# Lag and length of a scan's software pipeline: halves seven steps apart, outputs in step 11 of 13

## The chip, the cores and the metric

The kernel runs on one core of a Trainium2 chip. A core has TensorE (matrix products, into PSUM), VectorE, ScalarE and GpSimd (POOL in the profile), and SyncE, which here only issues the loads of weights. Each engine works through its own program in order; semaphores order the engines against each other. The metric is the device time of one execution in microseconds, lower is better.

## The reference

One hybrid layer over 512 tokens, then two layers over 512 + 256 tokens, all in float32. The hybrid layer mixes two kinds of attention with a gated linear attention (GLA). Each of the two later layers mixes a Fourier branch, an attention of 8 heads over 2 key-value heads, and a gated recurrence that runs forward and backward:

```python
def hgrn_scan(k, v, log_f, s0, q=None):
    # S_t = diag(f_t) S_{t-1} + k_t v_t^T, o_t = S_t^T q_t, chunk by chunk
    def step(s, inp):
        kc, vc, lf = inp[0], inp[1], inp[2]
        cum = jnp.cumsum(lf, axis=2)
        last = cum[:, :, -1:, :]
        s_new = jnp.exp(last[:, :, 0, :])[..., None] * s + \
            jnp.einsum('bhsd,bhse->bhde', kc * jnp.exp(last - cum), vc)
```

The outputs of a chunk are a part within the chunk (masked scores times values) and a part from the state that comes into it (queries times state).

## The kernel before

The program is a row of stages. The large products (`gemm_*`, matmuls at L654 and L657) fill most of the span. Between `in...` and `out...` products of each layer stands a stage in which two generators share the engines: the scan (`scan_pe`, `scan_act`, `scan_dve`) and the attention (`att_*`), in the two later layers followed by the Fourier branch (`four_*`). GpSimd runs its part of the attention alone, by semaphores.

How they are interleaved: `branch` keeps a position for each generator, always lets the one with the smaller position go on (the scan on a tie), and so writes one program for each engine before anything runs. A scan tick t of `ticks` yields (t+1)/(ticks+5) (five further ticks read and normalise the outputs); the attention of the later layers has 32 (layer 0) or 24 (layer 1) steps plus 4 and yields positions up to 0.8, and the Fourier part takes ten positions F0 to F9 from 0.8 to 1. The same positions are used on TensorE, ScalarE and VectorE.

The scan works on halves. The first stage (GLA) has one half, the later layers four each: two head pairs forward, two backward. A half goes through numbered steps k. `LAG` is the number of ticks between the start of a half and the start of the next, so in a tick step k of half n stands beside step k - LAG of half n+1. VectorE goes through the halves of a tick from the latest to the earliest (`reversed`), ScalarE and TensorE from the earliest on. The steps:

- k=0: VectorE floors the gate's input; ScalarE makes the logarithm of the gate in three or four passes (L1511, L1514, L1519 and in layer 1 L1523; `log`, `F`).
- k=1: VectorE's prefix sum (L1367 or L1369, `cum`) and `total`. It waits for `log`.
- k=2: VectorE makes the keys (L1380), the differences (L1383) and their clamp (L1385, `dif`); ScalarE then makes `decay` and two exponentials E0, E1 (L1531, L1533, `base_e`), waiting for `dif`.
- k=3 to 5: VectorE makes the factors of the scores, ScalarE further exponentials.
- k=6: TensorE's scores (L1604 to L1613); VectorE's `qi` and `ko` (`inter`).
- k=7: VectorE masks the scores; TensorE turns `ko` (L1621, `turned`); ScalarE copies it out as `k_tok` (L1548).
- k=8, 9: TensorE's updates (L1630) in k=8; VectorE links the chunk states (L1449), 12 links in k=8 and 11 in k=9, each waiting for the one before it.
- k=10: TensorE's outputs, the part within chunks (L1643) and the part from the states (L1649). They wait for the last link, `states`.
- k=11: VectorE copies the outputs out of PSUM (L1461, L1463).

An attention step s on TensorE (L1051, L1063 and L1084; here called step s) makes the transposed logits of step s in PSUM, waiting for the exponentials of step s-1 (L1233 on ScalarE), and then the values of step s-1; after the last step of a group it makes sums (L1101). VectorE's division by the sums (L1160) sets `weighted`, for which the Fourier part F0 on TensorE (L1749) waits.

Of the kernel before, what the change touches and what calls it, by code (L numbers as in the profile page):

```python
# [46 lines left out]
EXP_CAP = 85.0  # L47
SUB = 16
CH = 32
LAG = 6  # L50


COLS = {}
# [83 lines left out]
def blocks_kernel(nc, dram, out_t):  # L137
# [24 lines left out]
    with ExitStack() as ctx:  # L162
# [1162 lines left out]
        def blocks(t, b):  # L1325
            return t.rearrange("p (g b) -> p g b", b=b)

        def bank(i):
            return PS[2 + i // 2][:, 512 * (i % 2):512 * (i % 2) + 512]

        SCAN_TICKS = 12
        READ_TICKS = 5

        def scan_ticks(ss):
            n = sum(s.H for s in ss)
            return (n - 1) * LAG + SCAN_TICKS

# [3 lines left out]
        def scan_dve(v, st, ss):  # L1341
# [4 lines left out]
            def step(n, k):  # L1346
# [88 lines left out]
                if k in (8, 9):  # L1435
# [10 lines left out]
                    for i in range((k - 8) * m, min(len(links), (k - 7) * m)):  # L1446
# [3 lines left out]
                                                       bank(a_ % 4)[:, a_ // 4 * HD:a_ // 4 * HD + HD], ALU.mult, ALU.add).then_inc(tell.sem, 1)  # L1450
                        if tell is v_step:
                            v.wait_ge(v_step.sem, v_step.up())
                if k == 11:
                    v.wait_ge(S("outputs").sem, S("outputs").at(n + 1))
                    for w in range(s.R // 2):
                        dst = s.out(u + w)[:, 0:s.own].rearrange("p (t j c) -> p j t c", j=4, c=CH)
                        for j in range(4):
                            tell = S("out") if w == s.R // 2 - 1 and j == 3 else v_step
                            src = blocks(bank(j)[:, w * s.own // 4:(w + 1) * s.own // 4], CH)
                            if s.back:  # L1460
                                nc.vector.tensor_tensor(dst[:, j], src, dst[:, j], ALU.add).then_inc(tell.sem, 1)  # L1461
                            else:
                                nc.vector.tensor_copy(dst[:, j], src).then_inc(tell.sem, 1)  # L1463
                            if tell is v_step:
                                v_step.up()

            for tick in range(ticks):
                for n in reversed(range(len(hs))):
                    if 0 <= tick - LAG * n < SCAN_TICKS:
                        step(n, tick - LAG * n)  # L1470
                yield (tick + 1) / (ticks + READ_TICKS)
# [20 lines left out]
        def scan_act(a, st, ss):  # L1492
# [57 lines left out]
            for tick in range(ticks):  # L1550
                for n in range(len(hs)):
                    if 0 <= tick - LAG * n < SCAN_TICKS:
                        step(n, tick - LAG * n)
                yield (tick + 1) / (ticks + READ_TICKS)
# [23 lines left out]
        def scan_pe(p, st, ss):  # L1578
# [4 lines left out]
            def step(n, k):  # L1583
# [39 lines left out]
                if k == 8:  # L1623
# [7 lines left out]
                                              room["k_tok"][rows, P * t + s.dk * r:P * t + s.dk * r + s.dk],  # L1631
                                              s.v(t, s.R * u + r)[rows, :], start=True, stop=True)
                    mm.then_inc(S("updates").sem, 1)
                if k == 10:
                    p.wait_ge(S("states").sem, S("states").at(n + 1))
                    states = blocks(room["states"][:], HD)
                    att, qi = s.att(), s.parity("qi", n)
                    for t in range(s.n_out):
                        for j in range(4):
                            rows = slice(CH * j, CH * j + CH)  # L1640
                            for r in range(s.R):
                                o = (r // 2) * s.own // 4 + CH * t
                                mm = p.matmul(bank(j)[HD * (r % 2):HD * (r % 2) + HD, o:o + CH], s.v(t, s.R * u + r)[rows, :],  # L1643
                                              att[rows, r * s.nt * CH + CH * t:r * s.nt * CH + CH * t + CH],
                                              start=t == 0 and r < 2, stop=False)
                    def incoming(t, j, r, close):
                        o = (r // 2) * s.own // 4 + CH * t
                        c0 = P * t + CH * j
                        return p.matmul(bank(j)[HD * (r % 2):HD * (r % 2) + HD, o:o + CH], states[s.rows(r), 4 * t + j, :],  # L1649
                                        qi[s.rows(r), c0:c0 + CH], start=False, stop=close)  # L1650

                    if s.gla:
                        for turn_ in range(4):
                            mm.then_inc(p_step.sem, 1)
                            p.wait_ge(p_step.sem, p_step.up())
                            for t in range(s.n_out):
                                for r in range(s.R):
                                    mm = incoming(t, (r + turn_) % 4, r, t == s.n_out - 1 and turn_ >= 2)
                    else:
                        for t in range(s.n_out):  # L1660
                            for j in range(4):
                                for r in range(s.R):
                                    mm = incoming(t, j, r, t == s.n_out - 1)
                    mm.then_inc(S("outputs").sem, 1)

            for tick in range(ticks):
                for n in range(len(hs)):
                    if 0 <= tick - LAG * n < SCAN_TICKS:
                        step(n, tick - LAG * n)
                yield (tick + 1) / (ticks + READ_TICKS)  # L1670
# [548 lines left out]
```

## Time and profile before

| | |
|---|---|
| median of 3 runs | 2799.89 us (2788.68 to 2802.16) |
| the profiled execution | 2790.8 us, span 2788.7 us |
| TensorE busy | 2536.9 us, mean granted clock 0.935 |
| VectorE, ScalarE, GpSimd busy | 849.7, 793.6, 780.8 us |
| the stages with a scan | about 270 to 396, 1113 to 1318 and 2158 to 2347 us of the span |

A timeline row gives the start, the duration of the row's instructions together, the engine, the line, what is written from what, and in brackets how long the engine had been idle before and what ended that. The waits view sums such idle times by pair. The windows view gives the busy time of each engine in a stretch and the granted TensorE clock, 1.00 being full speed (2.4 GHz) and 0.50 the lower level (1.2 GHz).

### The profile page before, as it was taken

Reading aid. Unit: us, or ns where it says so; the run is one execution under the profiler, and the core shown is the slowest. Engines: PE = TensorE matmul, PEld = TensorE weight load, DVE = VectorE, ACT = ScalarE, POOL = GpSimd, SP = SyncE. Lnnn points to the kernel's source line nnn. Section 1 sums busy time; section 2 is a strip of 40 time slices with the busy share of each in tenths; the row PEclk is TensorE's granted clock in tenths of the full one; section 3 lists DMA queues with packets and bytes.
Section 4 is the critical chain, followed back from the end, with each engine's and each line's share of the span. In section 5 each row is a group of like instructions: output and inputs, shape, how many; then the busy total and the mean of one; then the engine's idle time right before and its main releaser. Section 6 shows DMA issues by size and latency. Waiting matters only on the chain.

```text
span 2788.7 us, 38017 instructions
## 1 busy us (share of the span) xinstructions
PE 2536.9 (91%) x16714; PEld 1950.0 (70%) x16714; DVE 849.7 (30%) x1287; ACT 793.6 (28%) x1007; POOL 780.8 (28%) x262
## 2 busy tenths in 40 slices
PE   4998888999999999987989999999799878899998
PEld 3876556777776678345878888888568335678786
DVE  3002336342344541662231111111441553311113
ACT  3122233221223421533232112112432533322222
POOL 1232133333332210410222222222221321344432
PEclk9898799999999999988999999999999778999999
DMA  6541013443343110101111112111110102222221
GB/s 178 140 150 69 17 61 129 155 178 151 151 181 113 55 39 1 45 3 61 61 46 63 58 63 74 58 56 46 70 46 8 45 2 89 78 91 91 91 98 53
DMA packets 42952, 220.52 MB, mean 79 GB/s; under 512 B 4072, under 2 KB 12920, under 8 KB 19492
## 3 DMA queue, kind: packets, MB, share of 16 engines
q1 hardware_dynamic: 35624, 200.52, 19.6%
q10 hardware_dynamic: 7164, 17.57, 2.5%
q8 instruction: 132, 2.16, 0.3%
q14 instruction: 32, 0.26, 0.0%
HBM read 212.05 MB, written 6.03 MB: 78 GB/s over the span
## 4 chain that ended last, share of the span: by engine, by line
PE 75%; DVE 7%; ACT 2%; issue 1%; POOL 0%; DMA 0%; ACTq 0%; DVEq 0%; POOLq 0%
PE PS L654 58%; PE PS L657 2%; PE PS L1051 2%; PE PS L1084 2%; DVE s_states L1449 2%; DVE tmp L587 1%; DVE a_lo L579 1%; PE PS L715 1%; PE PS L1649 1%; PE PS L1757 1%; PE PS L1848 1%; DVE hid_lo L868 1%; PE PS L1101 1%; PE PS L1063 1%; PE PS L537 1%
## 5 line engine op out<-in xcount | busy, mean ns | idle before, releaser
L1966 POOL TENSOR_TENSOR w_lo<-raw,w_hi 128x2048 fp32r<-128x2048 f32 (+2 forms) x146 | 649.7, 4450 | 1653.3 <-ACT w_hi L751 1653.3
L654 PE MATMUL PS<-a_hi,w_hi 128*128 128x512 f32 (+1 forms) x2104 | 694.4, 374 | 88.8 <-DVE a_lo L579 58.3
L654 PE MATMUL PS<-a_lo,w_hi 128*128 128x512 f32 (+1 forms) x2104 | 674.9, 365 | 0.0
L654 PE MATMUL PS<-a_hi,w_lo 128*128 128x512 f32 (+1 forms) x2104 | 673.8, 365 | 0.0
L654 PEld LDWEIGHTS PS<-a_hi,w_hi 128*128 128x128 f32 x2104 | 361.6, 191 | 184.4 <-issue 114.8
L654 PEld LDWEIGHTS PS<-a_lo,w_hi 128*128 128x128 f32 x2104 | 361.2, 191 | 63.3 <-issue 0.7
L654 PEld LDWEIGHTS PS<-a_hi,w_lo 128*128 128x128 f32 x2104 | 359.7, 190 | 65.4
L751 ACT ACTIVATE w_hi<-raw 128x2048 fp32r<-128x2048 f32 (+2 forms) x146 | 270.6, 1853 | 390.6 <-PE PS L654 202.8
L654 PE MATMUL PS<-hid_hi,w_hi 128*128 128x512 f32 (+1 forms) x784 | 265.6, 375 | 29.6 <-DVE hid_lo L868 29.6
L654 PE MATMUL PS<-hid_lo,w_hi 128*128 128x512 f32 (+1 forms) x784 | 263.9, 373 | 0.0
L654 PE MATMUL PS<-hid_hi,w_lo 128*128 128x512 f32 (+1 forms) x784 | 263.7, 373 | 0.0
L865 DVE TENSOR_TENSOR tmp<-PS,sq 128x768 f32<-128x768 f32 (+1 forms) x44 | 36.3, 825 | 481.7 <-PE PS L654 481.7
L654 PEld LDWEIGHTS PS<-hid_hi,w_hi 128*128 128x128 f32 x784 | 138.4, 193 | 63.7 <-issue 38.4
L1189 POOL TENSOR_TENSOR acc<-acc,pt 128x512 f32<-128x512 f32 (+3 forms) x100 | 116.9, 1169 | 213.7 <-PE PS L1084 154.9
L654 PEld LDWEIGHTS PS<-hid_hi,w_lo 128*128 128x128 f32 x784 | 138.6, 193 | 25.7
L654 PEld LDWEIGHTS PS<-hid_lo,w_hi 128*128 128x128 f32 x784 | 138.1, 192 | 24.7
L803 ACT ACTIVATE hid_hi<-tmp 128x512 fp32r<-128x512 f32 (+1 forms) x76 | 52.9, 696 | 355.4 <-DVE tmp L865 248.2
L851 DVE SCALAR_TENSOR_TENSOR x<-PS,mods,x 128x512 f32<-128x512 f32 x64 | 48.1, 751 | 313.5 <-PE PS L654 313.4
L868 DVE TENSOR_TENSOR hid_lo<-tmp,hid_hi 128x512 fp32r<-128x512 f32 (+1 forms) x76 | 102.9, 1354 | 67.7 <-ACT hid_hi L803 67.7
L1051 PE MATMUL PS<-proj 64*128 64x512 f32 (+3 forms) x208 | 104.3, 673 | 16.9 <-ACT acc L1233 13.2
L657 PE MATMUL PS<-w_hi,a_hi 128*128 128x256 f32 (+1 forms) x352 | 103.9, 295 | 3.4 <-POOL w_lo L1966 3.4
L657 PE MATMUL PS<-w_hi,a_lo 128*128 128x256 f32 (+1 forms) x352 | 102.5, 291 | 0.0
(203 smaller groups left out, 2478.9 us busy)
## 6 DMA issues: line engine op xcount, KB each, us to landing
raw<-in_w_ada SPq DMA_DIRECT2D x48, 1024.0 KB, 6.9
raw<-in_w_ff SPq DMA_DIRECT2D x32, 1024.0 KB, 4.7
raw<-in_w_in SPq DMA_DIRECT2D x27, 1024.0 KB, 4.8
raw<-in_w_gate SPq DMA_DIRECT2D x22, 1024.0 KB, 4.7
raw<-in_w_up SPq DMA_DIRECT2D x22, 1024.0 KB, 4.7
raw<-in_w_down SPq DMA_DIRECT2D x16, 1024.0 KB, 4.8
raw<-in_w_out SPq DMA_DIRECT2D x12, 1024.0 KB, 5.6
raw<-in_w_down SPq DMA_DIRECT2D x8, 768.0 KB, 4.2
```

The source lines that it names most:

```text
L654: mm = p.matmul(ps[:, dst], wv[:, k, idx * P:(idx + 1) * P], av[:, k, dst], start=first, stop=last)
L657: mm = p.matmul(ps[:, 0:ncol], av[:, k, idx * P:(idx + 1) * P], wv[:, k, 0:ncol], start=first, stop=last)
L751: nc.scalar.activation(w_hi[:, m % 2, 0:kt, 0:ncol], raw[:, i % 3, 0:kt, 0:ncol], ACT.Copy).then_inc(s_hi.sem, 1)
L803: nc.scalar.activation(hid_hi[:, tile, span(parts)], tmp[:, h % 2, span(parts)], ACT.Copy).then_inc(s_hhi.sem, 1)
L851: nc.vector.scalar_tensor_tensor(dst[:, tile, own], ps[:, src], mods[:, l, o, c:c + 1], dst[:, tile, own], ALU.mult, ALU.add).then_inc(tel ...
L865: nc.vector.tensor_tensor(tmp[:, h % 2, sp_], ps[:, sp_], sq[:, tile % 2, sp_], ALU.mult).then_inc(s_relu.sem, 1)
L868: nc.vector.tensor_tensor(hid_lo[:, tile, sp_], tmp[:, h % 2, sp_], hid_hi[:, tile, sp_].bitcast(F32), ALU.subtract).then_inc(low.sem, 1)
L1051: p.matmul(turned_ps(m)[:, lo:n], hd["k"][:, P * j:P * (j + 1)], hd["q"][:, grp["c0"] + lo:grp["c0"] + n], start=True, stop=False)
L1084: mm = p.matmul(values_ps(plan, g)[hd["rows"], lo:n], hd["v"][j], exps(plan, s, h, lo, n), start=first, stop=last)
L1189: pool.tensor_tensor(total_, total_, pt[:, s % 2, h, lo:n], ALU.add).then_inc(S("added").sem, 1)
L1449: nc.vector.scalar_tensor_tensor(states[:, b_, :], states[:, a_, :], s.room[f"decay{n % 2}"][:, a_:a_ + 1], bank(a_ % 4)[:, a_ // 4 * HD:a ...
L1966: pool.tensor_tensor(w_lo[:, m % 2, 0:kt, 0:ncol], src, w_hi[:, m % 2, 0:kt, 0:ncol].bitcast(F32), ALU.subtract).then_inc(s_lo.sem, 1)
```

## The change

`LAG` goes from 6 to 7 and `SCAN_TICKS` from 12 to 13. TensorE's outputs move from step 10 to step 11, VectorE's copy of them from step 11 to step 12; step 10 is then empty for a half. All other steps keep their numbers. The ticks of the later layers go from 3 x 6 + 12 = 30 to 3 x 7 + 13 = 34, those of the first stage from 12 to 13.

```diff
-LAG = 6
+LAG = 7
...
-        SCAN_TICKS = 12
+        SCAN_TICKS = 13
         READ_TICKS = 5
...
-                if k == 11:
+                if k == 12:
                     v.wait_ge(S("outputs").sem, S("outputs").at(n + 1))
                     for w in range(s.R // 2):
...
-                if k == 10:
+                if k == 11:
                     p.wait_ge(S("states").sem, S("states").at(n + 1))
                     states = blocks(room["states"][:], HD)
```

## Rows read from the trace of the kernel before

**Rows 1.** The page, busy time, share and count of TensorE and weight loads

```profile
PE 2536.9 (91%) x16714; PEld 1950.0 (70%) x16714; DVE 849.7 (30%) x1287; ACT 793.6 (28%) x1007; POOL 780.8 (28%) x262
```

**Rows 2.** Windows: stretch, length, busy by engine, clock; layer 0 and layer 1 stages

```profile
1113.00:1318.00 205.00, 174.65 (x2616) 88.56 (x2616) 105.73 (x197) 83.66 (x140) 51.32 (x33) 0.84 0.09 32
2158.00:2347.00 189.00, 149.55 (x1897) 69.54 (x1895) 90.79 (x194) 76.94 (x122) 47.75 (x33) 0.77 0.09 34
```

**Rows 3.** Waits of TensorE in layer 1's stage: us in total, times, longest

```profile
PE PS L1643 <- DVE s_states L1449: 23.9, 4, 8.0
...
PE PS L1630 <- ACT s_k_tok L1548: 0.9, 1, 0.9
```

**Rows 4.** The same waits in layer 0's stage

```profile
PE PS L1643 <- DVE s_states L1449: 8.0, 2, 7.8
```

**Rows 5.** Timeline of TensorE, layer 1, from half 1's turned to its outputs

```profile
2224.92 1.03 PE L1101 MATMUL PS<-acc,ones 128*64 128x512 f32 x4
...
2226.74 0.87 PE L1621 MATMUL PS<-ident,s_ko 128*128 128x128 f32 x6
...
2230.10 1.25 PE L1630 MATMUL PS<-tok,s_k_tok 32*64 32x64 f32 x96
...
2233.78 0.69 PE L1051 MATMUL PS<-proj,k_swap 64*128 64x512 f32 x1
...
2235.55 1.08 PE L1084 MATMUL PS<-pt,tok 128*64 128x512 f32 x4
2241.91 1.18 PE L1643 MATMUL PS<-s_att,tok 32*64 32x32 f32 x64 [5.29 <-DVE s_states L1449]
...
2246.58 1.22 PE L1051 MATMUL PS<-proj,k_swap 64*128 64x512 f32 x1
...
2251.22 1.22 PE L1051 MATMUL PS<-proj,k_swap 64*128 64x512 f32 x1
```

**Rows 6.** Timeline of VectorE in the same stretch

```profile
2223.96 1.76 DVE L1367 TENSOR_TENSOR_SCAN s_X<-s_lf_pad,reset 128x768 f32<-128x768 f32 x1 [4.63 <-ACT s_lf_pad L1523]
...
2226.27 1.01 DVE L1380 SCALAR_TENSOR_TENSOR proj<-proj,lbs,s_F 128x768 f32<-128x768 f32 x1
...
2228.19 0.56 DVE L1385 TENSOR_SCALAR s_d<-s_d 128x768 f32<-128x768 f32 x1
...
2231.49 3.76 DVE L1449 SCALAR_TENSOR_TENSOR s_states<-s_states,s_decay,PS 128x64 f32<-128x64 f32 x12 [2.67 <-PE PS L1630]
...
2238.43 3.44 DVE L1449 SCALAR_TENSOR_TENSOR s_states<-s_states,s_decay,PS 128x64 f32<-128x64 f32 x11
```

**Rows 7.** Timeline of ScalarE in the same stretch

```profile
2220.17 0.84 ACT L1511 ACTIVATE proj<-proj 128x768 f32<-128x768 f32 x1
...
2222.90 1.03 ACT L1523 ACTIVATE s_lf_pad<-s_F,lbs 128x768 f32<-128x768 f32 x1
...
2227.65 0.81 ACT L1548 ACTIVATE s_k_tok<-PS 128x768 f32<-128x768 f32 x1 [2.40 <-PE PS L1621]
2228.35 0.59 ACT L1240 ACTIVATE inverse<-PS 128x512 f32<-128x512 f32 x1
...
2231.32 0.84 ACT L1533 ACTIVATE s_E<-s_d 128x768 f32<-128x768 f32 x1
2232.93 1.09 ACT L1233 ACTIVATE pt<-PS 128x512 f32<-128x512 f32 x2 [0.77 <-PE PS L1063]
```

**Rows 8.** Timeline of TensorE in layer 0, the outputs of half 0

```profile
1167.16 1.17 PE L1643 MATMUL PS<-s_att,tok 32*64 32x32 f32 x96 [0.24 <-DVE s_states L1449]
```

**Rows 9.** Timeline of TensorE in layer 0, the same matmuls at two times

```profile
1236.64 1.12 PE L1101 MATMUL PS<-acc,ones 128*64 128x256 f32 x4 [3.15 <-DVE proj L1160]
...
1242.36 0.60 PE L1101 MATMUL PS<-acc,ones 128*64 128x256 f32 x4
```

**Rows 10.** Timeline of layer 0's end: last division on VectorE, first Fourier tiles on TensorE

```profile
1269.90 0.42 DVE L1160 TENSOR_TENSOR proj<-PS,inverse 128x256 f32<-128x256 f32 x1
...
1280.54 6.45 PE L1749 MATMUL PS<-f_feat,proj 128*128 128x256 f32 x20
```

## The prediction

> **What bounds the kernel now.** I read the page first: TensorE is busy 91% of the span [rows 1], so a gain or a loss must be TensorE idle time or TensorE clock. The windows by stage show where both are poor: in the two stages in which attention and the two-layer scan run side by side, TensorE is idle for 30 and 39 us and its granted clock is 0.84 and 0.77 [rows 2]. The diff touches nothing outside the scan stages. The waits of TensorE say why: in the layer 1 stage four waits for the state chain L1449 make 23.9 us [rows 3]; in layer 0 there are two, 8.0 us [rows 4]. The timeline of one half shows the shape [rows 5]: turned, an attention step, updates, two more steps, then 5.29 us idle until the outputs. I write A13 for attention step 13. A step takes 2.8 us at full clock (2233.78 to the end of the row at 2235.55); the outputs and the steps behind them run at half clock, 4.64 us a step (2246.58 to 2251.22).
>
> **What the change does to the order.** `branch` takes whichever generator stands earlier; a scan step is worth 1/(ticks+5) of the stage. Ticks go from 30 to 34, so a scan step is worth 1/39 instead of 1/35 and fewer attention steps lie between two of them. Merging by hand gives, for half 1 of layer 1:
> before: outputs0, A10, A11, scores1, A12, turned1, A13, updates1, A14, A15, outputs1;
> after: outputs0, A10, A11, scores1, A12, turned1, updates1, A13, A14, A15, outputs1.
> So against attention the outputs do not move at all; turned or updates come one attention step earlier, and three steps instead of two cover the states. This is the gain one would look for. Layer 0 is alike (updates one step earlier in halves 0 and 1, four steps cover; half 2 unchanged). Last half of both layers: the outputs come behind F0 and F1 (first two Fourier tiles) instead of ahead of them.
>
> The lag does more. Step k of half n now meets step k-7 of half n+1, not k-6. Three pairs matter.
> (a) ScalarE, step 7: the copy of k_tok, which waits for turned, now stands ahead of the next half's logarithm passes (k=0), which used to be a step earlier.
> (b) VectorE, step 8: the next half's prefix sum (k=1), which waits for that logarithm, stands ahead of the first 12 state updates.
> (c) VectorE steps 8 and 9, ScalarE step 9: the next half's k=2 (keys, difference, clamp) used to run before the first 12 states; now it runs behind them. ScalarE's exponentials of that difference stand ahead of the attention exponentials of the same place, and TensorE's attention step after that needs those.
>
> **The chain, from rows.** Let T be the end of turned. Layer 1: k_tok copy 0.9 with its latency; the logarithm passes 3.7 (2220.17 to 2223.93) [rows 7]; prefix sum and total 2.0 (2223.96 to the keys' turn) and 0.2 to start, so states begin at T+6.8; 12 states 3.8; k=2 is 2.5 (2226.27 to the end of the clamp, 2228.75) [rows 6]: T+13.1; two exponentials 1.6 (one is 0.84, they overlap by 0.1) and the first head's attention exponential 0.6 [rows 7]: T+15.3; then one whole attention step 2.8: outputs at T+18.1. The other 11 states end at T+16.6, so the old wait is gone and the attention exponential has taken its place. That ScalarE really keeps this order shows in the trace: the `inverse` pass at 2228.35 had its input when the sums ended, before turned, but ran only after the k_tok copy that stands ahead of it and waited 2.40 us [rows 7].
>
> The Trainium skill says the same of the queue (TensorE: Matmul & The Clock Gate, "Architectural detail: the array is 16× 32×32, not 1× 128×128": ScalarE and VectorE are strict FIFO, only TensorE pulls weight loads ahead). By that rule nothing ready on ScalarE passes the waiting exponential, and the sum below stands; if it could pass, the sum would be that of the first rival.
>
> Layer 1, each half against before, at full clock:
> - half 0: T+18.1; before, A6 with its sums (1.8 from 2224.92 to the turned, less what the step gives up to them: 4.4 in all) and then 14.3 (turned to outputs) [rows 5]: 18.7. -0.6 us.
> - half 1: T+18.1; before 14.3 (2227.6 to 2241.91) [rows 5] with the same three steps. +3.8 us. TensorE would idle 0.9 for k_tok, the price of that copy when no step covers it [rows 3], and some 7.2 ahead of A15.
> - half 2: 18.8 (the division L1160 falls between the two lots of states, 0.7) against 14.3+2.8 for one more step done. +1.7 us.
> - half 3: F0 and F1 fill 2.6 us (1.3 a tile [rows 10]) of the wait for states. They cannot start before the last `weighted`, which lies between the two lots of states as in layer 0 [rows 10], so 4 to 5 us of idle time stay. Later the squares stand behind F3 instead of F2, and about 1 us is given back. -1.8 us.
> Sum +3.1 us.
>
> Layer 0: the logarithm is ready after two of the passes (1.8), the attention exponentials after three. Half 0: states begin at T+5.0, the exponential that TensorE needs is there at T+13.5, TensorE stands ready at T+9.8 and idles 3.7; with A11, A12 and its sums (4.5) outputs at T+20.8 against 16.6 before, where the wait was only 0.24 [rows 8]. +4.2 us. Half 1: sums lie in A18, before the stall, so it is 2.0: +2.8 us. Half 2 shares its wait with a 3.15 us wait for the division [rows 9]: +0.7. Tail, F0 and F1: -1.2. Sum +6.5 us. The bound from below for these stalls is 0 (if work shown as VectorE's were earlier), from above 2.5 us more each (k=2 at twice its time).
>
> The first stage (one half, 12 to 13 ticks): scores before A7 instead of A8, outputs before A14 instead of A13. No next half, so none of (a) to (c). Its outputs did not wait for states, VectorE's masks keep their place, attention goes on after the scan's end. I put 0; if the cover fails one such wait as elsewhere, up to +2.
>
> No DMA moves: SP's loads behind the scan wait for the same last product, and the rest of the Fourier part lies between that product and the first matmul that needs them; if that cover failed, the loss would be the tail's 1 to 2 us. GpSimd's adds follow the exponentials and are late with them; their consumer, the sums, lies a step or more behind.
>
> **Clock.** A stall is not only its length. After 5.29 us idle the outputs and two steps ran at the lower of the two levels, 1.2 GHz, each step 1.8 us longer [rows 5]; after 3.15 us idle four matmuls took 1.12 instead of 0.60, and by 1242 the clock was back [rows 9]. Layer 0 gets two stalls (3.7, 2.0) where it had none: 2 steps more at the lower level. In layer 1 the stall moves ahead of one attention step, which then runs slow ahead of the outputs: likely for two of three halves. Four steps at 1.8 make +7 us. Ends: 0 and +16 (nine steps).
>
> Sum: 3.1 + 6.5 + 7.2 = +16.8 us, 0.6%.
>
> **Rivals.**
> 1. The cover works: the exponentials are not held up, the states' wait in layer 1 falls from 5.29 to 2.5 three times (-8.4) and the clock holds for outputs and two steps in each (-5 each), -23 us. For it: 23.9 us of waits on the very chain that gets more cover. Against: VectorE's and ScalarE's own program order. It decides where k=2 of the next half is done before TensorE has finished the second step after the updates; by the rows it is 8 us late. Ends faster. 0.08.
> 2. Stalls as computed, but the clock gives them back: layer 0 already loses a long stretch at the lower level (stage clock 0.84 [rows 2]) without a long idle time at its start, and stalls elsewhere may shift such stretches away. +0 to +8 us, no measurable change. 0.22.
> 3. The stalls take the whole clock in each half, and VectorE is slowed in k=2: +27 to +40 us. 0.10.
> 4. The merge is not as I have it: if the outputs did move by a step, +-3 us around rival 2; counted there.
>
> **How the numbers follow.** Forecast +16.8 (own range +8 to +27): 0.60, of which 0.42 beyond 0.5% (14 us, about what a measurement of this kernel tells from no change) and 0.18 within. Slower 0.42+0.10 = 0.52; same 0.18+0.22 = 0.40; faster 0.08. The profiled execution took 2790.8; the median of the three runs is 2799.9, 9 above. From the one, 2807.6, from the other 2816.7: I take the middle, 2812. Range: from about -3 us on the middle of the two (2792) to rival 3's middle (2836 is +41 on it, or +36 on the median).
>
> **What would show it.** In the profile after: the waits for L1449 at L1643 fall from 23.9 us to under 8 in the layer 1 stage, while waits of attention's matmuls at L1051 for ScalarE's exponentials appear, over 15 us in the two stages, the longest (about 7) ahead of A15 in layer 1; ScalarE idle at L1531 for the clamp L1385, and VectorE's L1369/L1367 directly ahead of each first lot of states. The layer 1 stage is some 3 to 9 us longer, layer 0 some 6 to 13. Wrong if L1051 does not wait, if stage clocks rise above 0.84 and 0.77, or if the first stage moves by over 2 us.

## The result and the profile after

The changed kernel takes 2823.13 us (median, 2813.83 to 2826.52), the kernel before in the same comparison 2797.78 us: 25 us between the medians, and a recorded ratio of 1.0095 with the 95% interval 1.0061 to 1.0129. The profiled execution took 2813.8 us (span 2812.1) against 2790.8 (2788.7), which is 23.4 us more. The page, its line of busy times, is answered by [rows 1]:

```profile
PE 2549.9 (91%) x16714; PEld 1949.1 (69%) x16714; DVE 854.7 (30%) x1287; ACT 793.3 (28%) x1007; POOL 781.5 (28%) x262
```

TensorE's 13 us more of busy time are the same 16714 matmuls at a lower clock. The windows of the three scan stages (columns as in [rows 2]), each from its activation table's load to the first large product behind it; first the kernel before, cut at the same two events, then the changed one:

```profile
235.60:398.50 162.90, 129.80 (x1203) 81.16 (x1203) 54.67 (x165) 48.48 (x96) 45.34 (x49) 0.82 0.07 23
1113.00:1318.60 205.60, 174.65 (x2616) 88.57 (x2617) 106.33 (x198) 84.26 (x141) 51.32 (x33) 0.84 0.09 33
2159.00:2347.20 188.20, 149.06 (x1892) 69.19 (x1893) 90.97 (x194) 76.86 (x121) 47.75 (x33) 0.76 0.09 34
```
```profile
233.40:404.60 171.20, 134.36 (x1203) 83.57 (x1203) 55.05 (x165) 48.66 (x96) 45.59 (x49) 0.80 0.07 22
1116.40:1333.07 216.67, 179.85 (x2617) 88.60 (x2617) 105.65 (x198) 83.99 (x141) 51.31 (x33) 0.84 0.09 31
2174.30:2369.03 194.73, 153.97 (x1892) 69.85 (x1893) 96.64 (x194) 78.56 (x123) 48.41 (x33) 0.76 0.09 33
```

The stages are 8.3, 11.1 and 6.5 us longer, 25.9 together. The stretches ahead of, between and behind them differ by -2.2, -2.7, +0.8 and +1.6 us. Length less busy time is TensorE's idle time: 33.1 to 36.8, 31.0 to 36.8 and 39.1 to 40.8 us, 11.2 us more in all. The other 14.7 us are the same matmuls taking longer. So in this pair of profiles more than half of the loss is clock.

The waits of TensorE in the layer 1 stage of the changed kernel (us in total, times, longest), which answer [rows 3]:

```profile
PE PS L1051 <- ACT pt L1233: 13.1, 3, 4.7
PE PS L1051 <- ACT acc L1233: 5.2, 1, 5.2
PE PS L1084 <- ACT inverse L1240: 5.1, 2, 3.6
PE PS L1749 <- DVE proj L1160: 4.8, 1, 4.8
```

The 23.9 us for the states are gone: L1643 waits 1.3 us for L1449 in the whole execution. In their place stand 13.1 us for attention exponentials (L1051 for `pt`), 5.1 for the inverse of the sums and 4.8 for the last division. (The 5.2 us for `acc` stand at the stage's start in both kernels.) In layer 0, where [rows 4] had 8.0 us:

```profile
PE PS L1051 <- ACT acc L1233: 6.8, 2, 4.3
PE PS L1051 <- ACT pt L1233: 6.6, 4, 4.2
PE PS L1749 <- DVE proj L1160: 4.5, 1, 4.5
PE PS L1101 <- DVE proj L1160: 3.2, 1, 3.2
```

Of these, 4.3 of the 6.8 us for `acc` and the 3.2 us of L1101 stand in the kernel before too; the other 2.5 us for `acc` and the 6.6 us for `pt` are new, and the 4.5 us of L1749 stand where 7.8 us for the states stood.

How half 1 of layer 1 goes now. TensorE, from turned to the outputs (against [rows 5]):

```profile
2240.09 0.87 PE L1621 MATMUL PS<-ident,s_ko 128*128 128x128 f32 x6
2241.87 1.25 PE L1630 MATMUL PS<-tok,s_k_tok 32*64 32x64 f32 x96 [0.90 <-ACT s_k_tok L1548]
...
2246.08 1.92 PE L1084 MATMUL PS<-acc,tok 128*64 128x512 f32 x4 [1.47 <-ACT inverse L1240]
...
2256.00 1.22 PE L1051 MATMUL PS<-proj,k_swap 64*128 64x512 f32 x1 [4.70 <-ACT pt L1233]
...
2261.12 1.18 PE L1643 MATMUL PS<-s_att,tok 32*64 32x32 f32 x64
2262.23 3.63 PE L1649 MATMUL PS<-s_qi,s_states 64*64 64x32 f32 x64
```

The outputs come 20.2 us after turned ended (2240.96), where it was 14.3 before. They wait for nothing; the stall has moved up and stands in three places, the longest of them directly ahead of the last attention step. VectorE in the same stretch (against [rows 6]) has the next half's keys, L1380, and clamp, L1385, behind the 12 states instead of ahead of them:

```profile
2245.48 1.76 DVE L1367 TENSOR_TENSOR_SCAN s_X<-s_lf_pad,reset 128x768 f32<-128x768 f32 x1 [9.00 <-ACT s_lf_pad L1523]
2247.58 3.76 DVE L1449 SCALAR_TENSOR_TENSOR s_states<-s_states,s_decay,PS 128x64 f32<-128x64 f32 x12
2251.38 1.02 DVE L1380 SCALAR_TENSOR_TENSOR proj<-proj,lbs,s_F 128x768 f32<-128x768 f32 x1
...
2253.30 0.56 DVE L1385 TENSOR_SCALAR s_d<-s_d 128x768 f32<-128x768 f32 x1
2253.78 3.44 DVE L1449 SCALAR_TENSOR_TENSOR s_states<-s_states,s_decay,PS 128x64 f32<-128x64 f32 x11
```

ScalarE (against [rows 7]) makes the k_tok copy, then the four logarithm passes, then the inverse whose sums have long been there, and after one more pair of attention exponentials it waits 6.16 us for the clamp, with the next pair queued behind:

```profile
2241.00 0.81 ACT L1548 ACTIVATE s_k_tok<-PS 128x768 f32<-128x768 f32 x1 [2.39 <-PE PS L1621]
...
2245.36 0.58 ACT L1240 ACTIVATE inverse<-PS 128x512 f32<-128x512 f32 x1
...
2253.89 0.84 ACT L1531 ACTIVATE s_E<-s_d 128x768 f32<-128x768 f32 x1 [6.16 <-DVE s_d L1385]
2254.64 0.83 ACT L1533 ACTIVATE s_E<-s_d 128x768 f32<-128x768 f32 x1
2255.37 1.06 ACT L1233 ACTIVATE pt<-PS 128x512 f32<-128x512 f32 x2
```

### The profile page after: what moved, and what is told of

Its sections match the earlier page's. It is cut to its first block, busy times and chain, and to the rows that moved or that the text cites. A ratio compares the mean times of both kernels' runs of the same rounds, so it can differ in the third digit from the quotient of the medians.

```text
span 2812.1 us, 38021 instructions
## 1 busy us (share of the span) xinstructions
PE 2549.9 (91%) x16714; PEld 1949.1 (69%) x16714; DVE 854.7 (30%) x1287; ACT 793.3 (28%) x1007; POOL 781.5 (28%) x262
## 4 chain that ended last, share of the span: by engine, by line
PE 74%; DVE 7%; ACT 3%; issue 2%; POOL 0%; DMA 0%; ACTq 0%; DVEq 0%; POOLq 0%
PE PS L654 57%; PE PS L657 2%; PE PS L1051 2%; PE PS L1084 2%; DVE tmp L587 1%; DVE a_lo L579 1%; PE PS L715 1%; DVE s_states L1449 1%; PE PS L1757 1%; PE PS L1848 1%; PE PS L1649 1%; DVE hid_lo L868 1%; PE PS L537 1%; PE PS L1101 1%; PE PS L1063 1%
## 5 line engine op out<-in xcount | busy, mean ns | idle before, releaser
L654 PEld LDWEIGHTS PS<-a_hi,w_hi 128*128 128x128 f32 x2104 | 360.5, 191 | 185.4 <-issue 115.0
L1051 PE MATMUL PS<-proj 64*128 64x512 f32 (+3 forms) x208 | 106.8, 692 | 30.9 <-ACT acc L1233 16.9
```

What stands on the lines that cost most here:

```text
L654: mm = p.matmul(ps[:, dst], wv[:, k, idx * P:(idx + 1) * P], av[:, k, dst], start=first, stop=last)
L1051: p.matmul(turned_ps(m)[:, lo:n], hd["k"][:, P * j:P * (j + 1)], hd["q"][:, grp["c0"] + lo:grp["c0"] + n], start=True, stop=False)
```

## The experiments

My theory: what costs is the order that the lag makes on ScalarE and VectorE, above all the next half's keys and clamp (k=2) behind the first 12 states, and not the later outputs. The rival: stalls are paid back by the clock, or the outputs' own step matters. The table sets the runs side by side. Stage lengths and clocks are of one profiled execution each; the ratio to the kernel before is the recorded one, with its 95% interval; it differs from the quotient of the two medians by up to 0.0012. The kernel before was run anew beside e1 to e4, e5 to e8, and e9 with e10, so kernels of two such groups compare less sharply than two of one.

| kernel | ratio | first stage, us | layer 0, us (clock) | layer 1, us (clock) |
|---|---|---|---|---|
| before | 1 | 162.9 | 205.6 (0.84) | 188.2 (0.76) |
| changed | 1.0095 (1.0061 to 1.0129) | 171.2 | 216.7 (0.84) | 194.7 (0.76) |
| the changed one again (e9_changed) | 1.0105 (1.0068 to 1.0141) | 169.7 | 230.4 (0.79) | 196.8 (0.75) |
| e8_lag_only | 1.0110 (1.0060 to 1.0161) | 165.8 | 228.6 (0.79) | 193.4 (0.78) |
| e1_outputs_only | 1.0040 (1.0014 to 1.0065) | 169.4 | 218.7 (0.82) | 175.2 (0.81) |
| e2_act_order | 1.0068 (1.0038 to 1.0098) | 173.1 | 213.8 (0.85) | 188.9 (0.75) |
| e3_k2_early | 1.0011 (0.9985 to 1.0038) | 169.5 | 203.0 (0.87) | 184.2 (0.80) |
| e4_both | 0.9917 (0.9886 to 0.9949) | 166.1 | 202.8 (0.84) | 162.9 (0.85) |
| e5_first_only | 1.0027 (1.0004 to 1.0051) | 170.6 | 209.6 (0.83) | 185.4 (0.79) |
| e6_first_old | 1.0117 (1.0072 to 1.0161) | 163.2 | 227.0 (0.78) | 197.2 (0.74) |
| the same again (e10_first_old) | 1.0079 (1.0052 to 1.0105) | 164.4 | 217.0 (0.85) | 196.3 (0.77) |
| e7_all | 0.9895 (0.9858 to 0.9932) | 159.2 | 200.2 (0.89) | 163.0 (0.85) |

**The lag alone** (on the kernel before):

```diff
-LAG = 6
+LAG = 7
```

> Halves seven steps apart, outputs left in step 10 of 12 (the first stage is then as before). Theory: pairs (a) to (c) are all there. In layer 1 only A7 and A8 stand between updates and outputs of half 0, so TensorE waits for the exponential or the states as before and again after the outputs: L1643 waits 5 to 9 us for L1449 and L1051 for ScalarE 1 to 3 us. Two-layer stages at least as long as in the changed kernel: ratio 1.004 to 1.012. Rival (the loss comes from the later outputs): ratio 0.998 to 1.002.

Measured: 1.0110. The lag alone has the whole loss, and the rival (0.998 to 1.002) is out. Waits of TensorE in its layer 1 stage:

```profile
PE PS L1643 <- DVE s_states L1449: 26.1, 4, 9.7
...
PE PS L1084 <- ACT inverse L1240: 3.6, 1, 3.6
```

With the outputs in their old step, the states' wait does not fall but rises (23.9 to 26.1 us): the states themselves are late, since VectorE's prefix sum and ScalarE's logarithm now stand ahead of them. The stage of layer 1 is as long as in the changed kernel (193.4 against 194.7), and so moving the outputs has only changed the name of the wait there. Parts of the expectation failed: the longest wait for the states is 9.7 us (5 to 9 was said), and L1051 waits 0.4 us in all for `pt` there (1 to 3 was said).

**The outputs alone** (on the changed kernel):

```diff
-LAG = 7
+LAG = 6
```

> Halves six steps apart as before, but the outputs in step 11 of 13: the later outputs without the lag. Theory (order of the programs): the next half's k=2 runs ahead of the first 12 states as before, so ScalarE's exponentials are in time; in layer 1 three attention steps cover the states, the wait for L1449 falls from 5.29 us to about 2.5 in each of three halves, and no attention matmul (L1051) waits over 2 us for ScalarE's L1233 except at the stage's start. Layer 1's stage 8 to 20 us shorter than before. The first stage as in the changed kernel (its outputs moved, +10 us). Rival (the later outputs themselves cost, whatever the lag): both two-layer stages as long as in the changed kernel, ratio 1.009. Theory's ratio 0.994 to 1.000.

Waits of TensorE, first in its layer 1, then in its layer 0 stage:

```profile
PE PS L1643 <- DVE s_states L1449: 8.7, 4, 2.5
...
PE PS L1749 <- DVE proj L1160: 4.8, 1, 4.8
```
```profile
PE PS L1749 <- DVE proj L1160: 7.9, 1, 7.9
...
PE PS L1101 <- DVE proj L1160: 6.4, 1, 6.4
```

In layer 1 this is what the cover was to bring: the wait for states falls from 23.9 to 8.7 us, the attention steps wait 0.5 us in all for `pt`, the clock rises to 0.81 and the stage is 13.0 us shorter. But the whole is 1.0040, outside the 0.994 to 1.000 that was expected, and not faster: the first stage is 6.5 us longer, and layer 0 13 us longer, of which 7.0 are idle time (31.0 to 38.0). There the wait of L1101 for a division is 6.4 us, where it was 3.15 in the kernel before [rows 9], and L1051 waits 2.5 us for `acc` at 1177.30, where it did not wait. The 7.9 us of L1749 stand where 7.8 us for the states stood. Why the division came later was not followed up. That the outputs' step alone makes the kernel faster fell; that the lag, and not the outputs, holds up layer 1 stands.

**ScalarE's order put back** (on the changed kernel, in `scan_act` alone: the later half goes first, so the logarithm passes run ahead of the k_tok copy again):

```diff
-                for n in range(len(hs)):
+                for n in reversed(range(len(hs))):
```

> The changed kernel, but ScalarE goes through the halves of a tick from the latest to the earliest, so the next half's logarithm passes stand ahead of the k_tok copy that waits for turned. Theory: pairs (a) and (b) vanish, states start at the end of the updates (U) instead of 4.5 us after turned's end plus prefix sum; pair (c) stays: the attention exponential behind k=2 comes at U+8.5, so TensorE idles about 3 us (half 0) to 3 us (half 1) in layer 1 instead of 4.3 and 4.7 plus 1.5. Time some 6 to 12 us under the changed kernel, still not under the kernel before. Rival (the logarithm has nothing to do with it): no change from 1.009.

Measured: 1.0068. In layer 1 the wait for the inverse is gone and the wait for k_tok has grown from 1.8 to 2.9 us (longest 2.0). The wait of L1051 for `pt` is 12.5 us instead of 13.1. So pairs (a) and (b) by themselves are a small part, and the main stall is not ScalarE's own order but the clamp that comes late to it: ScalarE's wait for it (L1531) in this stage is 15.8 us, where it is 17.5 in the changed kernel and nothing in the kernel before. The gain on the changed kernel, 0.3%, is what was expected (6 to 12 us), but it is inside the two intervals.

**The keys and the clamp with the prefix sum** (on the changed kernel, in `scan_dve` alone, for all three stages):

```diff
-                if k == 2:
+                if k == 1:
```

> The changed kernel, but VectorE does the next half's k=2 (keys, difference, clamp) together with its k=1, ahead of the first 12 states. Theory: pair (c) vanishes, (a) and (b) stay: states begin 2.5 us later (turned's end + 9.3), all states at + 16.6, outputs there instead of + 18.1 to 20.4; the wait is again one for L1449 at L1643, 3 to 7 us, the waits at L1051 for ScalarE under 2 us each. Some 4 to 10 us under the changed kernel. Rival (k=2 is not what ScalarE waits for): L1051 goes on waiting over 4 us.

Measured: 1.0011, no longer distinguishable from the kernel before (the medians are 6.4 us apart, about what the first stage costs, as shown below). The waits of TensorE in its layer 1 stage:

```profile
PE PS L1084 <- ACT inverse L1240: 5.1, 2, 3.6
PE PS L1749 <- DVE proj L1160: 4.8, 1, 4.8
PE PS L1643 <- DVE s_states L1449: 4.4, 2, 2.2
...
PE PS L1051 <- ACT pt L1233: 3.9, 2, 2.8
```

The wait for `pt` falls from 13.1 to 3.9 us (the longest is 2.8, where under 2 was said); 4.4 us of waits for states come back, since states now wait for the k=2 work. The stage is 10.5 us shorter, layer 0's 13.7. This one edit takes back nearly all of the change's loss, so pair (c) is its main cause. The gain is some 20 us, where 4 to 10 were expected. It is more than the stalls alone are worth: of the 10.5 us in layer 1, 4.7 are idle time (40.8 to 36.1).

**Both orders:** the two edits above together.

> Both: ScalarE's order turned and k=2 early. Theory: states begin at the end of the updates, three attention steps (8.4 us) stand against some 7.3 us of states in layer 1, so neither L1051 nor L1643 waits over 1.5 us in halves 0 to 2, and the clock falls less often. Two-layer stages together 20 to 40 us shorter than in the changed kernel and 10 to 25 shorter than before; the first stage keeps its +10. Ratio 0.990 to 1.000. Rival (the clock falls for other reasons than these waits): waits vanish, stage clocks stay at 0.76 to 0.84 and the time is at 1.000 to 1.005.

Measured: 0.9917, faster than the kernel before (medians 2767.74 and 2790.37 us). The windows of its layer 0 and layer 1 stages:

```profile
1116.10:1318.90 202.80, 175.15 (x2617) 86.83 (x2617) 108.25 (x198) 84.03 (x141) 54.17 (x33) 0.84 0.09 33
2154.50:2317.40 162.90, 136.15 (x1892) 62.62 (x1893) 93.57 (x194) 77.97 (x123) 48.76 (x33) 0.85 0.10 40
```

Layer 1 is 31.8 us shorter than in the changed kernel, of which 14.0 are idle time (40.8 to 26.7) and 17.8 are matmuls at a higher clock. The two edits alone gained 5.8 and 10.5 us there. They are worth more together, in idle time (4.6 and 4.7 us alone, 14.0 together) as in clock. ScalarE's wait for the clamp in this stage shows how: 17.5 us in the changed kernel, 15.8 with its own order turned, 7.9 with the keys early, and 2.2 with both. The clamp needs the logarithm, and it needs to stand ahead of the states; each edit alone mends one of the two. With the keys' edit alone, ScalarE still waits 4.19 us for the clamp in half 1, TensorE waits 2.78 us, and the outputs run at half clock (1.2 GHz); first ScalarE's row, then TensorE's:

```profile
2241.49 0.84 ACT L1531 ACTIVATE s_E<-s_d 128x768 f32<-128x768 f32 x1 [4.19 <-DVE s_d L1385]
...
2243.61 1.22 PE L1051 MATMUL PS<-proj,k_swap 64*128 64x512 f32 x1 [2.78 <-ACT pt L1233]
...
2248.87 1.18 PE L1643 MATMUL PS<-s_att,tok 32*64 32x32 f32 x64
```

With both orders ScalarE does not wait for the clamp in this half, and the outputs wait 0.36 us and run at full clock. The row is from the last kernel here, which has both orders and the old first stage, and 0.40 us:

```profile
2217.72 0.86 PE L1643 MATMUL PS<-s_att,tok 32*64 32x32 f32 x64 [0.40 <-DVE s_states L1449]
```

What stays in this half is a wait of 2.02 us for k_tok ahead of the updates, the price of ScalarE's order. The gain was larger than expected: the two stages together are 45.7 us shorter than in the changed kernel (20 to 40 was said) and 28.1 shorter than before (10 to 25).

**The first stage.** It was the one stage that I had put at nothing. Step 11 for the outputs in the first stage alone, on the kernel before (`scan_ticks` gives one tick more for a single half, and the tick loops run one step further for it):

```diff
-                if k == 11:
+                if k == (12 if s.gla else 11):
...
-                if k == 10:
+                if k == (11 if s.gla else 10):
```

> The kernel before with only the first stage (GLA, one half) changed: its outputs in step 11 of 13, its copy in step 12; the later layers as before. Theory from the two traces: the outputs and the means stood behind the sums (L1101) and covered the 1.84 us that ScalarE needs for the inverse and the next exponential; moved, L1051 waits 1.84 us for ScalarE's acc twice more (7.4 us in four times instead of 3.7 in two) and the clock falls. First stage 4 to 11 us longer, ratio 1.001 to 1.004. Rival (the 10.7 us between the two profiled first stages are the clock of one execution): the two waits appear, but the ratio is 0.999 to 1.001.

and the opposite on the changed kernel, step 10 in the first stage alone, `- int(n == 1)` in `scan_ticks`:

```diff
-                if k == 12:
+                if k == (11 if s.gla else 12):
...
-                if k == 11:
+                if k == (10 if s.gla else 11):
```

> The changed kernel with the first stage as before: outputs of the GLA half in step 10 of 12. Theory: 4 to 11 us under the changed kernel, ratio 1.005 to 1.008, the waits of L1051 for ScalarE's acc in the first stage back at 3.7 us. Rival (the first stage costs nothing on the median): ratio 1.009 as the changed kernel.

Measured: 1.0027 (7.8 us between the medians) for the first; its interval is clear of 1, but not of the rival's 1.001. The second missed its expectation: 1.0117, which by itself says that putting the outputs back brings nothing. In its profile the first stage is 8.0 us shorter than the changed kernel's, but its layer 0 stage, which is the same program (exponential waits of 4.4 us where the changed kernel has 6.6), ran at clock 0.78 and took 227.0 us. One profile does not explain a median of five runs, so both went once more, side by side:

> The changed kernel again, beside the next run on the same chip, since the medians left open whether the first stage has a share of the loss. Expected ratio to before 1.008 to 1.012, layer 1's stage 194 to 197 us, layer 0's 214 to 230 us with the same waits (only the clock between them).

> The changed kernel with the first stage as before, beside the changed kernel on the same chip. Theory (the moved outputs and means uncovered 1.84 us twice in the first stage, some 7 us with the clock): first stage 160 to 166 us instead of 167 to 173, median 4 to 10 us under the changed kernel of the same call. Rival (given back later): the first stage is shorter, the medians are within 2 us.

Measured: 2822.57 us (1.0105) for the changed kernel, 2813.53 (1.0079) with the old first stage, 9.0 us apart, as expected (4 to 10); but the intervals of the two ratios overlap widely, and with e6_first_old beside them the share of the first stage in the whole time is not shown on the changed kernel. Here it was the changed kernel's profiled execution whose layer 0 stage ran slowly (230.4 us, 0.79, at the edge of the 214 to 230 that was said), and that of the other did not. The length of the first stage itself is clearer. Over all profiled executions it sorts without an overlap, by 0.3 us: with the outputs where they were 162.9, 163.2, 159.2, 165.8 and 164.4 us, mean 163.1; one step later 171.2, 169.7, 169.4, 173.1, 169.5, 166.1 and 170.6, mean 169.9. That is 6.8 us between the means.

The timeline of TensorE shows how. The kernel before:

```profile
333.94 1.08 PE L1101 MATMUL PS<-acc,ones 128*64 128x512 f32 x4 [0.62 <-DVE small L1140]
...
334.95 1.82 PE L1643 MATMUL PS<-s_att,tok 32*64 32x32 f32 x128
```

The changed kernel:

```profile
334.35 2.13 PE L1051 MATMUL PS<-proj 64*128 64x384 f32 x4 [1.84 <-ACT acc L1233]
...
364.09 1.40 PE L1051 MATMUL PS<-proj 64*128 64x384 f32 x4 [1.84 <-ACT acc L1233]
```

Behind the sums (L1101), the next attention step waits for an exponential that ScalarE makes only after the two passes of the inverse of those sums (L1240, L1242). Before, the outputs stood between the sums and that step and hid it, and the scan's means (L1680) hid it a second time at 364. One step later, neither stands there. The waits of L1051 for `acc` in this stage are 7.4 us in four places instead of 3.7 in two, and in these two profiles the clock of the stage falls from 0.82 to 0.80. In the run of the first stage alone they are 7.4 us as well, in that with the old first stage 3.7.

**All of it:** both orders and the old first stage.

> ScalarE's order turned, k=2 early, and the first stage as before. Theory: the gain of the two orders (ratio 0.992) and 4 to 11 us from the first stage: ratio 0.988 to 0.991. Rival (the first stage costs nothing): 0.992.

Measured: 0.9895 (2762.4 us), the fastest of all and faster than both kernels beyond the intervals. Its layer 1 stage is as with both orders, its first stage the shortest. How much the first stage adds to that (0.0022) is less than the two intervals can tell. What is left in its layer 1 stage, besides the 5.2 us at its start:

```profile
PE PS L1749 <- DVE proj L1160: 4.9, 1, 4.9
...
PE PS L1630 <- ACT s_k_tok L1548: 2.9, 2, 2.0
PE PS L1643 <- DVE s_states L1449: 2.3, 3, 1.4
```

So a kernel with the lag of 7 is faster than the one before, once the order inside a tick is fitted to it: the cover that was to hide the states is real, and VectorE and ScalarE had used it up on the next half. That the lag itself is needed for this is not shown. The two orders were not tried with a lag of 6, where e1_outputs_only already has the cover in layer 1 (175.2 us).

## Why the prediction was right, and where it was not

It said 2812 us (2792 to 2836), slower by 0.6%, from program order on VectorE and ScalarE. Measured were 2823, slower by 0.95%, and in the second comparison 2823 again, slower by 1.05% (30 us between the medians). Step by step:

- **Order of the steps.** As merged by hand for half 1: turned, updates, three attention steps, outputs; in the last half F0 and F1 ahead of the outputs, and 4.8 us of idle time ahead of F0, where I had 4 to 5.
- **The chain of layer 1.** In half 0, turned ended at 2200.26, which is T. States began at T+6.6 (6.8 predicted), the clamp ended at T+13.1 (13.1), the attention step began at T+15.2 (15.3). From there the step took 5.1 us instead of 2.8, at half clock, and outputs came at T+20.3. I had put this slow step into the clock's term, so the T+18.1 of the text is this chain without it.
- **Where the stall lies.** In half 1 I had 0.9 us for k_tok and one stall of some 7.2 us ahead of A15, 8.1 in all. It was three: 0.90 for k_tok, 1.47 for the inverse and 4.70 for the exponential, 7.07 in all. The inverse stands in the same queue that I had cited for it and is held up by the logarithm passes, which I did not follow through. In half 2 it is 3.62 us, beside 4.09 us for the exponential. The longest exponential wait was 4.70 and not about 7. In e10_first_old it was 6.9.
- **Layer 0.** 4.16 us idle in half 0 for 3.7 predicted. In half 1 2.46 for 2.0, but for `acc`. A wait of 2.00 us for `pt` at 1142.46, ahead of half 0's scores, stands in no term of the sum; e6_first_old, the same program in this stage, does not have it.
- **Sum of the two stages.** Predicted 9.6 us of order and 7.2 us of clock. Measured 7.5 us of idle time (31.0 to 36.8, 39.1 to 40.8) and 10.1 us of longer matmuls, 17.6 for 16.8. Layer 1 +6.5 (3 to 9 was said), layer 0 +11.1 (6 to 13), stage clocks at 0.84 and 0.76, not above what they were. That it comes out so closely is in part luck, since the compared profile is the fastest of those with this program in both stages. Over all profiled executions with unchanged code in these stages (two of the program before, four of the changed one) layer 0 is 15.2 us longer (mean 207.6 to 222.8) and layer 1 9.4 (186.8 to 196.2), both beyond what was said. The two stages were put too low by some 8 us, and the runs do not say how much of that is order and how much clock.
- **What would show it.** L1643 waits 1.3 us for L1449 (under 8 was said), L1051 for `pt` 13.1 and 6.6 us (over 15), ScalarE 6.16 us for the clamp at L1531, and the prefix sum stands directly ahead of the first states.
- **The step that failed** is the first stage, put at 0, with +2 if the cover failed, and the text said that a move of over 2 us there would make it wrong. It is +6.8 us, mean against mean of the table, +8.3 in the two profiles. I had looked at what the scan waits for, not at what the outputs stand in front of. Two waits of 1.84 us had been hidden by them and by the means, and 4.6 of the 8.3 us are longer matmuls. With it the sum of 16.8 becomes 23.6; that the two profiles differ by 23.4 is luck, by the means of the two other stages. The medians differ by 25 and 30 us.
- **The range.** Its upper end, 2836, is called the middle of the third rival, but lies 41 us above the number it is counted from, beyond that rival's +40. The result is inside the range either way.
- **The rivals.** The first (the cover works) is refuted for this change and true of the mended one. The price I gave it, -23 us for layer 1, is near the 25.3 us by which that stage is shorter with both orders than before. The second (the clock gives it back) did not happen: the interval of the ratio begins above 1.005. Its own reason, that the clock of layer 0 moves without a wait to match, fits the last section, but no run tested it. The third was put at +27 to +40 us. The differences of the medians, 25 and 30 us, lie just below and just inside it, and both intervals reach into it. Half of its reason is refuted: the clamp's work on VectorE was not slowed, 2.5 us (2251.38 to 2253.86) as before. The other half, stalls that take more of the clock than I reckoned, is open.

The Trainium skill (TensorE: Matmul & The Clock Gate, "Architectural detail: the array is 16× 32×32, not 1× 128×128") says that ScalarE and VectorE are strict FIFO. The trace agrees twice: the inverse, whose sums had ended at about 2240.2, ran at 2245.36, and the exponentials of the attention step ran only behind L1531 and L1533.

What stays open: how a stage's loss divides between order and clock in any one run, as the clock of one execution moved the layer 0 stage by 10 to 14 us with nearly the same waits.

## What to carry to other kernels

When the lag of a software pipeline changes, write down for each in-order engine which steps of the next item change places with a step that waits; a step moved away from a wait is paid for by what is put in front of it. Mend the order within the tick before judging the lag: lag 7 gave 1.0095 as it came and 0.9895 with two orders changed and the first stage left alone. Try the orders at the old lag too, which was left out here. And before a block of ready work is moved, look at what the engine would wait for if it were not there.

## What the runs showed of the hardware

The clock of the layer 0 stage differs from execution to execution of one program. The changed kernel ran it in 216.7 us at 0.84 and, the second time, in 230.4 us at 0.79, with nearly the same waits of L1051 (6.8 and 6.7 us where the first has 6.8 and 6.6); e6_first_old and e10_first_old, one program too, took 227.0 at 0.78 and 217.0 at 0.85. One profile therefore does not tell 10 us in this stage; medians and the named waits do.

Half clock can follow a short wait as it follows a long one. In e7_all TensorE ran at full clock until a wait of 1.35 us, and the outputs behind it ran at half clock:

```profile
2185.96 1.06 PE L1643 MATMUL PS<-s_att,tok 32*64 32x32 f32 x64 [1.35 <-DVE s_states L1449]
2186.95 3.62 PE L1649 MATMUL PS<-s_qi,s_states 64*64 64x32 f32 x64
...
2197.33 1.08 PE L1084 MATMUL PS<-pt,tok 128*64 128x512 f32 x4
```

The four L1084 matmuls are back at 1.08 us some 11 us later. In e1_outputs_only each of three waits of 2.49 us for the states in layer 1 was followed by four L1084 matmuls at 1.98 us. In the changed kernel the wait of 1.47 us ahead of 2246.08 slowed TensorE for under 4 us (L1063 is back at 0.50 us at 2249.79), and the one of 4.70 us for about 19 (the L1084 matmuls still take 1.98 us at 2273.15):

```profile
2273.15 1.98 PE L1084 MATMUL PS<-pt,tok 128*64 128x512 f32 x4
```

What decides between the 4, the 11 and the 19 us was not tried.
